# The prompt's last 24 rows at other places of VectorE's order, and another order of the sample's rounds

## The chip, the cores and the metric

One core of one Trainium2 chip runs the whole program. The metric is the device time in microseconds of one execution. The kernel before takes 2661.11 us, the median of three runs (2660.18 to 2662.83). The execution that was profiled took 2656.66 us, of which 2654.9 lie between its first and its last instruction.

## The reference, cut to what matters

One encoder layer is applied to a prompt of 256 tokens and to a sample of 512 tokens: grouped-query attention and a spatial gating unit side by side, cross attention to 256 memory rows, and then a feed-forward layer of 16384 experts, each of them one row of 1024 numbers. In each of 8 heads a token picks 16 experts out of a product of two lists of 128 keys, by two rankings:

```python
def one_block(xb):
    q = (xb @ w_q).reshape(n, PEER_HEADS, PEER_D_KEY)
    q1, q2 = jnp.split(q, 2, axis=-1)
    s1 = jnp.einsum('nhd,hkd->nhk', q1, sub_k1)        # 128 scores
    s2 = jnp.einsum('nhd,hkd->nhk', q2, sub_k2)        # 128 scores
    v1, i1 = lax.top_k(s1, 16); v2, i2 = lax.top_k(s2, 16)
    cand = v1[..., :, None] + v2[..., None, :]         # 16 x 16
    top_s, top_c = lax.top_k(cand.reshape(n, 8, 256), 16)
    idx = e1 * 128 + e2                                # the keys of top_c
    g = softmax(top_s)
    act = gelu(einsum('nhkd,nd->nhk', e_down[idx], xb))
    return einsum('nhk,nhkd->nd', g * act, e_up[idx])
```

Everything is float32, on matrix products as three products of a high and a low part.

## The kernel before, in words

Tokens lie in six tiles of 128: tiles 0 and 1 are the prompt, 2 to 5 the sample. The layer runs twice, first for the prompt, then for the sample, and then the experts of both run together. Each pass has the same stages: `mixer_inputs` (eleven column blocks), `self_attention`, `mixer_outputs` (three products of two column blocks each), `cross_inputs`, `cross_attention`, and the routing, for the sample `routing_and_gates`. Weights come in halves of a column block; ScalarE makes the high part of each (`split_hi`, L211, tile w_hi) and VectorE the low part (`split_lo`, L219, tile w_lo), for which TensorE waits. Every engine has its order of instructions written out by hand; nothing plans it at run time.

The prompt's tokens and one tile of the sample get their expert rows by gathering. The sample's other three tiles go through all 16384 experts densely, with a table of gates, "dense gates".

**The rows.** For the prompt there are 256 gathered rows of the down table, one for each of the 128 places of a token's lists and each of the two tiles, for the 128 tokens of a tile at once (512 KB). The class `Rows` holds a ring of `K = 9` slots. GpSimd asks for row r with an indirect DMA (L148) once row r - 9 has been used; VectorE takes a row with one dot product of 1024 columns for each token (L136). `bg.dve(dve, n)` puts the next n rows at this place of VectorE's order, `bg.finish` all that are left. They stand in the sample's pass as filling, from the inputs' column block 5 on. `bg.pool` lets GpSimd ask as far ahead as nine rows beyond those that VectorE takes by the end of the same stage; in the routing the function `more_rows` counts it out. The prompt's ranking is done in part of the ring's memory, before the rows begin, and in the routing four slots of the ring take scores of the sample: ScalarE waits there for 251 used rows (L1721) before it copies the third block of scores.

**The rounds.** `pick_experts(r)` ranks for unit r of the list `order`, a pair of heads c (0 to 3) of a tile t (0 to 3), four lists of 128 scores (L1834 to L1849), and in the same round ranks the candidates of unit r - 1. GpSimd adds up the candidates of a unit and looks up the keys. The scores of pair c for all four tiles come from TensorE after the query block c and are copied by ScalarE (L1714). Tiles 1, 2, 3 are the dense ones, tile 0 is gathered. When the last unit of a tile has been ranked, `shift` (L1884, L1885), an exponential on ScalarE and `finish` (L1891 to L1893) make its gates; TensorE then turns the tile (`turn_pairs`, L1682), and the dense gates can be built. They are built in 48 steps of eight token columns: VectorE writes two masks (`stamp`, L1911 and L1916), ScalarE scales one of them (`gate`, L1746, eight instructions), TensorE multiplies (L1696), ScalarE moves the result out (`unload`, L1756, two instructions), and SP stores it. Stamps stand in rounds as `aside`, six in a full one and five in the last. The experts' stage (`experts`, L2019 and on) waits for the last unload and the last store.

`keep_busy` (L250) is work without a result on TensorE.

Of the kernel before, what the change touches and what calls it, by code (L numbers as in the profile page):

```python
# [33 lines left out]
ND = 3  # L34
# [550 lines left out]
def mixer_inputs(nc, block, st, q, bg, x_in, T, Y, qT, kT, v_sb, lin, tr, A, U, GA, GS, stage, ident, gains, choice=None, norm=None, routed=None):  # L585
# [4 lines left out]
    with ExitStack() as ctx:  # L590
# [131 lines left out]
        def _(dve):  # L722
# [63 lines left out]
            def aside(c, half):  # L786
                if not q.first:
                    r = {(0, 0): 3, (1, 0): 4, (3, 0): 5, (3, 1): 6, (4, 0): 7, (4, 1): 8}.get((c, half))
                    if r is not None:
                        choice.rank(dve, r)  # L790
                    if (c, half) == (4, 1):
                        choice.shift(dve)
                    if (c, half) == (SOFTEN, 1):
                        choice.finish(dve)
                    if (SOFTEN, 0) < (c, half) < (10, 1):
                        bg.dve(dve, 5)
# [324 lines left out]
def mixer_outputs(nc, block, st, q, bg, x_in, T, Y, G, lin, tr, A, U, GA, GS, ident, cleared, attended, spills_done):  # L1121
# [3 lines left out]
    with ExitStack() as ctx:  # L1125
# [99 lines left out]
        def _(dve):  # L1225
            def each(j, oo, use):
                for c in range(2):
                    h = H + 4 * j + 2 * c
                    bg.dve(dve, 4 if (j, c) == (2, 1) else 8)
                    st.split_lo(dve, h + 2)  # L1230
                    for t in range(NT):
                        n = c * NT + t
                        dve.wait_ge(oo.ready, n + 1)
                        s = NO * j + n
                        dve.wait_ge(side_in[s % RING], 16 * (s // RING + 1))
                        use(oo, n, t, slice(c * CH, (c + 1) * CH), side[:, s % RING, :])
                        if t < NT - 1:
                            bg.dve(dve, 1)
                    st.split_lo(dve, h + 3)
                    if j == 0 and c == 0:  # L1240
                        dve.wait_ge(small_in, 48)
                        norm.dve(dve, Y, sgn[:])
# [26 lines left out]
            turn_g.dve(dve)  # L1269
            norm_m.dve(dve, M)  # L1270
# [19 lines left out]
def cross_inputs(nc, block, st, q, bg, x_in, T, Y, G, keysT, vals, lin, tr, A, ident, gains, norm_m, mixed, cleared):  # L1290
    NT, H = q.nt, q.h0 + 2 * W_XKV
    X, Y = Y, Y[:, q.t0:q.t0 + NT, :]
    with ExitStack() as ctx:
# [67 lines left out]
        def _(dve):  # L1361
# [10 lines left out]
            for h in range(10, 14):  # L1372
                bg.dve(dve, 7 if h < 13 else 3)
                st.split_lo(dve, H + h)
# [161 lines left out]
def routing_and_gates(nc, block, st, q, bg, T, Y, G, H, E12, GATE, IDX, WD, lin, tr, A, ident, gains, attended):  # L1536
# [10 lines left out]
    with ExitStack() as ctx:  # L1547
# [12 lines left out]
        begun = bg.done  # L1560
# [47 lines left out]
        order = [(c, t) for c in range(NPC) for t in (1, 2)] + [(c, 3) for c in range(NPC)] + [(c, 0) for c in range(NPC)]  # L1608
# [4 lines left out]
        AFTER = {1: 2, 2: 4 * PER_UNIT, 3: ND * OCTS - 1}  # L1613

        EARLY, ROWS_XO, ROWS_FIRST = 3, 8, 14
# [166 lines left out]
        def _(dve):  # L1782
# [112 lines left out]
            def one_row():  # L1895
                bg.dve(dve, 1)

# [22 lines left out]
            bg.dve(dve, ROWS_FIRST)  # L1920
            assert all(st.is_loaded(H0 + h) for h in range(6, 12))
            for r in range(EARLY):
                pick_experts(r, one_row)
            bg.finish(dve)
            for r in range(EARLY, 8):
                pick_experts(r)
            shift(0)
            pick_experts(8)
            finish(0)
            for r in range(9, UNITS + 1):  # L1930
                if r == 9:
                    shift(1)
                pick_experts(r, stamp)
                if r == 9:
                    finish(1)
                if r == 12:
                    shift(2)
                if r == 13:
# [11 lines left out]
        def _(pool):  # L1950
# [7 lines left out]
            taken = begun + 2 * ROWS_XO + NT - 1 + ROWS_FIRST  # L1958

            def more_rows(n):  # L1960
                nonlocal taken
                taken += n
                bg.pool(pool, min(taken + bg.K, bg.end))

            more_rows(0)
            sums = 0
            for r in range(UNITS + 1):
                u = r
                if r == EARLY:
                    bg.pool(pool, bg.end)  # L1970
                if u < UNITS:
                    if r < EARLY:
                        more_rows(4)
# [10 lines left out]
                    if r < EARLY:  # L1984
                        more_rows(1)
                u = r - 1
                if u >= 0:
# [16 lines left out]
                    if r < EARLY:  # L2004
                        more_rows(1)
# [399 lines left out]
```

## Time and profile before

| | us |
|---|---|
| median of 3 runs | 2661.11 |
| the profiled execution: time | 2656.66 |
| the profiled execution: span | 2654.9 |
| TensorE, VectorE, ScalarE, GpSimd busy | 2429.2, 2222.1, 1105.6, 1366.6 |
| mean granted clock of TensorE | 0.977 of full speed |

By stretches of the profiled execution (busy us of each engine, and the granted clock of TensorE):

| stretch, us | TensorE | VectorE | ScalarE | GpSimd | clock |
|---|---|---|---|---|---|
| 850 to 900 | 46.06 | 37.77 | 19.01 | 23.91 | 0.97 |
| 900 to 950 | 49.38 | 46.64 | 9.77 | 32.16 | 1.00 |
| 950 to 1000 | 50.00 | 41.12 | 14.29 | 21.06 | 1.00 |
| 1050 to 1100 | 48.01 | 45.03 | 19.69 | 34.80 | 1.00 |
| 1100 to 1150 | 47.67 | 38.02 | 17.85 | 36.34 | 1.00 |
| 1200 to 1250 | 48.99 | 43.35 | 20.08 | 29.71 | 1.00 |
| 1250 to 1300 | 50.00 | 43.20 | 16.21 | 34.51 | 1.00 |
| 1300 to 1350 | 36.48 | 44.91 | 11.35 | 28.94 | 0.86 |
| 1350 to 1400 | 6.40 | 48.55 | 8.18 | 23.22 | 0.52 |
| 1400 to 1450 | 30.05 | 49.42 | 46.41 | 22.45 | 0.97 |
| 1500 to 1550 | 32.09 | 49.66 | 47.49 | 20.19 | 0.93 |

The sample's attention ends near 865, its cross attention near 1177, the routing's turn near 1235, the queries near 1340; the dense gates go from 1392 to 1565, and the experts' first product starts near 1571. An engine's busy time does not say what it waits for; the chain of waits and the rows in order of time do.

### The profile page before, as it was taken

The page shows a single profiled execution, that of the slowest core. Times are in us where ns is not written, and L with a number is a line of the kernel's source. Part 1 is how long each engine was busy: PE and PEld are TensorE (multiplying, and loading weights), DVE is VectorE, ACT ScalarE, POOL GpSimd, SP SyncE. Part 2 cuts the span into 40 slices and gives each one's busy share as a digit, 9 for nine tenths or more (in the row PEclk, how much of TensorE's full clock was granted, in tenths as well). Part 3 has the DMA queues.
Part 4 walks back from the last instruction along what each step waited for, and adds up shares of the span by engine and source line. Part 5 has one row for each costly group of instructions (what it writes and reads, how often), then busy time and mean ns, then how long its engine had stood idle before and what let it go on. Part 6 is the DMA issues. An engine that isn't in the chain of part 4 may idle for free.

```text
span 2654.9 us, 38615 instructions
## 1 busy us (share of the span) xinstructions
PE 2429.2 (92%) x13259; PEld 2108.0 (79%) x13259; DVE 2222.1 (84%) x3967; ACT 1105.6 (42%) x1938; POOL 1366.6 (51%) x1054
## 2 busy tenths in 40 slices
PE   7989999899999999999916669999999999999997
PEld 5767889788866788778715559999999999989997
DVE  6355545986688888877999979999999999999998
ACT  4463444333267223333219973333333333343333
POOL 0000000326722547746654447877777777767874
PEclk9999999999999999999968999999999999999999
DMA  6735535457954988968803369999999999999996
GB/s 244 277 120 202 182 134 217 153 205 292 377 203 121 339 302 306 349 220 315 324 0 128 161 272 413 414 415 410 402 402 403 402 404 404 402 394 386 415 414 247
DMA packets 235668, 781.18 MB, mean 294 GB/s; under 512 B 21376, under 2 KB 70576, under 8 KB 214800
## 3 DMA queue, kind: packets, MB, share of 16 engines
q0 software_dynamic: 112288, 408.77, 39.6%
q1 hardware_dynamic: 123248, 370.71, 37.3%
q8 instruction: 76, 1.25, 0.2%
q14 instruction: 56, 0.46, 0.0%
HBM read 724.87 MB, written 54.53 MB: 294 GB/s over the span
## 4 chain that ended last, share of the span: by engine, by line
PE 70%; DVE 17%; ACT 5%; DMA 3%; issue 3%; POOL 2%; SPq 0%; DVEq 0%; ACTq 0%; POOLq 0%
PE lin L242 15%; PE lin L243 15%; PE lin L244 15%; PE tr L242 7%; PE tr L243 6%; PE tr L244 6%; DVE row_ring L136 2%; DVE w_lo L219 2%; DVE w_hi L1911 2%; POOL row_ring L148 1%; DVE att_nmx L1104 1%; DVE mark L1916 1%; ACT row_ring L1746 1%; ACT w_hi L211 1%; DMA w_raw<-in_wall 1%
## 5 line engine op out<-in xcount | busy, mean ns | idle before, releaser
L148 POOL DMA_INDIRECT row_ring<-in_down,IDX x256 | 366.0, 1430 | 308.9 <-DVE dots L136 235.0
L219 DVE TENSOR_TENSOR w_lo<-w_raw,w_hi 128x2048 fp32r<-128x2048 f32 x100 | 230.0, 2300 | 227.1 <-ACT w_hi L211 207.3
L242 PE MATMUL lin<-w_hi,T_hi 128*128 128x512 f32 x976 | 391.2, 401 | 15.1 <-DVE w_lo L219 7.1
L243 PE MATMUL lin<-w_lo,T_hi 128*128 128x512 f32 x976 | 387.5, 397 | 0.0
L244 PE MATMUL lin<-w_hi,T_lo 128*128 128x512 f32 x976 | 387.3, 397 | 0.0
L211 ACT ACTIVATE w_hi<-w_raw 128x2048 fp32r<-128x2048 f32 x116 | 221.9, 1914 | 353.5 <-PE lin L244 313.4
L242 PE MATMUL tr<-T_hi,w_hi 128*128 128x384 f32 x1024 | 348.8, 341 | 3.1 <-DVE w_lo L2219 3.1
L244 PE MATMUL tr<-T_hi,w_lo 128*128 128x384 f32 x1024 | 345.7, 338 | 0.0
L243 PE MATMUL tr<-T_lo,w_hi 128*128 128x384 f32 x1024 | 345.3, 337 | 0.0
L2129 POOL DMA_INDIRECT rows<-in_up,now x192 | 298.2, 1553 | 85.9 <-issue 52.7
L136 DVE CUSTOM_DVE_ANT_0 row_ring<-row_ring,H 128x1024 f32<-128x1024 f32 x256 | 306.9, 1238 | 31.2 <-DMA row_ring<-in_down,IDX 26.9
L2129 POOL DMA_INDIRECT w_raw<-in_up,now x192 | 280.4, 1461 | 87.0 <-issue 42.8
L242 PE MATMUL lin<-w_hi,c_hi 128*128 128x512 f32 x768 | 301.0, 392 | 6.7 <-issue 4.9
L243 PE MATMUL lin<-w_lo,c_hi 128*128 128x512 f32 x768 | 300.1, 391 | 0.0
L244 PE MATMUL lin<-w_hi,c_lo 128*128 128x512 f32 x768 | 299.2, 390 | 0.0
L242 PEld LDWEIGHTS lin<-w_hi,T_hi 128*128 128x128 f32 x976 | 185.1, 190 | 60.7 <-DVE w_lo L219 8.9
L2177 ACT ACTIVATE w_hi<-row_ring 128x1024 fp32r<-128x1024 f32 x128 | 135.6, 1059 | 217.0 <-PE lin L244 214.4
L244 PEld LDWEIGHTS lin<-w_hi,T_lo 128*128 128x128 f32 x976 | 185.1, 190 | 44.3
L243 PEld LDWEIGHTS lin<-w_lo,T_hi 128*128 128x128 f32 x976 | 185.4, 190 | 42.8
L2185 ACT ACTIVATE gl<-tr 128x384 f32<-128x384 f32 x128 | 62.9, 491 | 364.1 <-PE tr L244 357.7
L2246 DVE SCALAR_TENSOR_TENSOR Y<-w_raw,dots,Y 128x1024 f32<-128x1024 f32 x160 | 201.9, 1278 | 4.2 <-DMA w_raw<-in_up,now 4.1
L2246 DVE SCALAR_TENSOR_TENSOR Y<-rows,dots,Y 128x1024 f32<-128x1024 f32 x160 | 201.8, 1277 | 1.4 <-DMA rows<-in_up,now 1.3
(291 smaller groups left out, 5256.5 us busy)
## 6 DMA issues: line engine op xcount, KB each, us to landing
w_raw<-in_wall SPq DMA_DIRECT2D x116, 1024.0 KB
G<-in_downT SPq DMA_DIRECT2D x128, 512.0 KB
row_ring<-in_up SPq DMA_DIRECT2D x128, 512.0 KB
wd<-dense_gates SPq DMA_DIRECT2D x32, 768.0 KB
weight_rests<-w_lo SPq DMA_DIRECT2D x16, 1024.0 KB, 4.8
w_lo<-weight_rests SPq DMA_DIRECT2D x16, 1024.0 KB
dense_gates<-peer SPq DMA_DIRECT2D x6, 2048.0 KB, 6.7
dense_gates<-w_raw SPq DMA_DIRECT2D x6, 2048.0 KB, 7.0
```

What stands on the lines that cost most here:

```text
L136: dve.tensor_tensor_reduce(self.ring[:, k, :], self.ring[:, k, :], self.H[:, r % 2, :], 1.0, 0.0, ALU.mult, ALU.add, self.dots[:, r:r + 1] ...
L148: pool.indirect_dma_start(self.ring[:, r % self.K, :], None, self.table, bass.IndirectOffsetOnAxis(ap=self.IDX[:, r:r + 1], axis=0)).then_ ...
L211: act.activation(self.hi[:, h % 2], self.raw[:, h % 2], ACT.Copy).then_inc(self.hi_done, 1)
L219: dve.tensor_tensor(self.lo[:, h % 2], self.raw[:, h % 2], self.hi[:, h % 2].bitcast(F32), ALU.subtract).then_inc(self.lo_done, 1)
L242: pe.matmul(out, lhs[0], rhs[0], start=start, stop=False, skip_group_check=True)
L243: pe.matmul(out, lhs[0], rhs[1], start=False, stop=False, skip_group_check=True)
L244: return pe.matmul(out, lhs[1], rhs[0], start=False, stop=stop, skip_group_check=True)
L1911: dve.tensor_tensor(hot2[:, r % 4], keys[:].unsqueeze(1).broadcast_to((P, OCT, NK)), pairs[:, i, 1, OCT * r:OCT * (r + 1)].unsqueeze(2).br ...
L2129: pool.indirect_dma_start(rows[k], None, table, bass.IndirectOffsetOnAxis(ap=now[:, j % 2, k:k + 1], axis=0)).then_inc(rows_in[k], 16)
L2177: act.activation(u_hi[:, b % 2], raw_u[:, b % RAW], ACT.Copy).then_inc(u_hid, 1)
L2185: act.activation(gl[:, b % 2, :], tr[:, b % 2, 0:DENSE], ACT.Gelu_apprx_tanh).then_inc(gelued, 1)
L2246: dve.scalar_tensor_tensor(out=into, in0=rows[k], scalar=dots[:, bass.ds(first_row + r, 1)], in1=into, op0=ALU.mult, op1=ALU.add).then_inc ...
```

## The change

Rows of the prompt are counted into VectorE's order at other places. By stage, rows taken before and after: inputs 50 and 55 (also in column block 10, second half), self attention 27 and 27, outputs 62 and 74 (twelve at first instead of eight, nine instead of eight in three of the other batches, and five more ahead of the memory's norm), cross inputs 44 and 49 (7, 9, 7, 6 in place of 7, 7, 7, 3 in the last four batches), cross attention 10 and 10, the routing up to its turn 19 and 21. What is left for the time after the turn is 44 rows before and 20 after. Before, 14 of the 44 stood ahead of round 0, 17 inside rounds 0 to 2, and 13 behind them; after, all 20 stand ahead of round 0, and GpSimd asks for all of them at once, with no requests between its look-ups.

The rounds take the units in another order. Before: (c, 1) and (c, 2) for all c, then (c, 3), then (c, 0). After, tile 3 of pairs 0 and 1 stands ahead of pairs 2 and 3 of tiles 1 and 2. So tile 1 is complete with unit 8 in place of unit 6, tile 2 with unit 9 in place of unit 7; tiles 3 and 0 as before. The first tile's gates are made after round 10 (before: round 8), and stamps stand in rounds 11 to 16 (before: 9 to 16), 35 of the 48 against 47, the rest behind the last round.

```diff
-                    if (SOFTEN, 0) < (c, half) < (10, 1):
+                    if (SOFTEN, 0) < (c, half):
                         bg.dve(dve, 5)
...
-                    bg.dve(dve, 4 if (j, c) == (2, 1) else 8)
+                    bg.dve(dve, {(0, 0): 12, (1, 1): 8, (2, 1): 4}.get((j, c), 9))
...
             turn_g.dve(dve)
+            bg.dve(dve, 5)
             norm_m.dve(dve, M)
...
-                bg.dve(dve, 7 if h < 13 else 3)
+                bg.dve(dve, {11: 9, 13: 6}.get(h, 7))
...
-        order = [(c, t) for c in range(NPC) for t in (1, 2)] + [(c, 3) for c in range(NPC)] + [(c, 0) for c in range(NPC)]
+        order = [(0, 1), (0, 2), (1, 1), (1, 2), (0, 3), (1, 3), (2, 1), (2, 2), (3, 1), (3, 2), (2, 3), (3, 3)] + [
+            (c, 0) for c in range(NPC)]
...
-        AFTER = {1: 2, 2: 4 * PER_UNIT, 3: ND * OCTS - 1}
-
-        EARLY, ROWS_XO, ROWS_FIRST = 3, 8, 14
+        AFTER = {1: 2, 2: 2 * PER_UNIT, 3: ND * OCTS - 1}
+
+        ROWS_XO = 9
...
-            bg.dve(dve, ROWS_FIRST)
+            bg.finish(dve)
             assert all(st.is_loaded(H0 + h) for h in range(6, 12))
-            for r in range(EARLY):
-                pick_experts(r, one_row)
-            bg.finish(dve)
-            for r in range(EARLY, 8):
+            for r in range(ROUTED[0] + 1):
                 pick_experts(r)
             shift(0)
-            pick_experts(8)
+            pick_experts(ROUTED[1])
             finish(0)
-            for r in range(9, UNITS + 1):
-                if r == 9:
-                    shift(1)
+            shift(1)
+            for r in range(ROUTED[1] + 1, UNITS + 1):
                 pick_experts(r, stamp)
-                if r == 9:
+                if r == ROUTED[1] + 1:
                     finish(1)
-                if r == 12:
+                if r == ROUTED[2]:
                     shift(2)
-                if r == 13:
+                if r == ROUTED[2] + 1:
                     finish(2)
             shift(3)
...
-            taken = begun + 2 * ROWS_XO + NT - 1 + ROWS_FIRST
-
-            def more_rows(n):
-                nonlocal taken
-                taken += n
-                bg.pool(pool, min(taken + bg.K, bg.end))
-
-            more_rows(0)
+            bg.pool(pool, bg.end)
```

## Rows read from the trace of the kernel before

**Rows 1.** The waits from 1236 to 1400 us: engine, line, releaser, us, times, longest.

```profile
PE lin L1682 <- DVE GATE L1893: 47.4, 1, 47.4
```

**Rows 2.** VectorE in order of time, 872 to 880: start, us, instruction, idle before it.

```profile
872.60 1.22 DVE L136 CUSTOM_DVE_ANT_0 row_ring<-row_ring,H 128x1024 f32<-128x1024 f32 x1
...
873.75 1.22 DVE L136 CUSTOM_DVE_ANT_0 row_ring<-row_ring,H 128x1024 f32<-128x1024 f32 x1
...
879.80 2.29 DVE L219 TENSOR_TENSOR w_lo<-w_raw,w_hi 128x2048 fp32r<-128x2048 f32 x1 [4.82 <-issue]
```

**Rows 3.** GpSimd in order of time, two requests eight apart, 1116 to 1134.

```profile
1116.66 1.91 POOL L148 DMA_INDIRECT row_ring<-in_down,IDX  x1 [0.30 <-issue]
...
1133.04 0.94 POOL L148 DMA_INDIRECT row_ring<-in_down,IDX  x1 [0.30 <-issue]
```

**Rows 4.** VectorE in order of time, in the cross queries, 1115 to 1138.

```profile
1115.47 2.29 DVE L219 TENSOR_TENSOR w_lo<-w_raw,w_hi 128x2048 fp32r<-128x2048 f32 x1 [1.28 <-ACT w_hi L211]
...
1126.20 1.23 DVE L136 CUSTOM_DVE_ANT_0 row_ring<-row_ring,H 128x1024 f32<-128x1024 f32 x1 [1.56 <-DMA row_ring<-in_down,IDX]
...
1137.75 2.29 DVE L219 TENSOR_TENSOR w_lo<-w_raw,w_hi 128x2048 fp32r<-128x2048 f32 x1 [4.68 <-issue]
```

**Rows 5.** VectorE in order of time, four places from 745 to 992.

```profile
745.90 2.29 DVE L219 TENSOR_TENSOR w_lo<-w_raw,w_hi 128x2048 fp32r<-128x2048 f32 x1 [6.90 <-ACT w_hi L211]
...
894.65 0.17 DVE L405 RECIPROCAL sg_rstd<-sg_sd 128x1 f32<-128x1 f32 x1 [1.32 <-ACT sg_sd L390]
...
942.66 2.29 DVE L219 TENSOR_TENSOR w_lo<-w_raw,w_hi 128x2048 fp32r<-128x2048 f32 x1 [1.55 <-ACT w_hi L211]
...
991.41 0.15 DVE L400 TENSOR_SCALAR mem_ms<-mem_ss 128x1 f32<-128x1 f32 x1 [6.90 <-ACT sg_squares L386]
```

**Rows 6.** GpSimd in order of time, one request at 875.

```profile
874.98 0.94 POOL L148 DMA_INDIRECT row_ring<-in_down,IDX  x1 [0.30 <-DVE dots L136]
```

**Rows 7.** TensorE in order of time, two places where it waited for VectorE.

```profile
917.80 2.38 PE L1190 MATMUL lin<-Y,sgw 128*128 128x512 f32 x5 [0.22 <-DVE G L1246]
...
1005.99 1.38 PE L250 MATMUL lin<-ident 128*128 128x128 f32 x10 [1.66 <-DVE w_lo L219]
```

**Rows 8.** VectorE in order of time, in the routing's first product, 1200 to 1215.

```profile
1200.64 1.22 DVE L136 CUSTOM_DVE_ANT_0 row_ring<-row_ring,H 128x1024 f32<-128x1024 f32 x1 [3.11 <-DMA row_ring<-in_down,IDX]
...
1214.16 2.29 DVE L219 TENSOR_TENSOR w_lo<-w_raw,w_hi 128x2048 fp32r<-128x2048 f32 x1
```

**Rows 9.** GpSimd in order of time, one request at 1210.

```profile
1210.37 1.99 POOL L148 DMA_INDIRECT row_ring<-in_down,IDX  x1 [0.30 <-issue]
```

**Rows 10.** TensorE in order of time, the routing's transposes.

```profile
1225.80 3.71 PE L336 MATMUL lin<-ident,G 128*128 128x128 f32 x32 [1.01 <-DVE G L408]
```

**Rows 11.** VectorE in order of time, the last rows and the rounds, 1267 to 1386.

```profile
1267.41 1.23 DVE L136 CUSTOM_DVE_ANT_0 row_ring<-row_ring,H 128x1024 f32<-128x1024 f32 x1 [0.25 <-DMA row_ring<-in_down,IDX]
...
1271.89 1.21 DVE L136 CUSTOM_DVE_ANT_0 row_ring<-row_ring,H 128x1024 f32<-128x1024 f32 x1
...
1326.54 0.87 DVE L1834 MAX8 best<-G 128x8 f32<-128x128 f32 x4
...
1336.06 0.87 DVE L1834 MAX8 best<-row_ring 128x8 f32<-128x128 f32 x4
...
1385.61 0.29 DVE L1891 TENSOR_REDUCE gsum<-GATE 128x8 f32<-128x128 f32 x1
```

**Rows 12.** ScalarE in order of time, the scores of pair 1, tile 1.

```profile
1285.22 0.60 ACT L1714 ACTIVATE G<-tr 128x512 f32<-128x512 f32 x1 [3.08 <-issue]
```

**Rows 13.** ScalarE in order of time, four of the 48 gates.

```profile
1391.92 2.45 ACT L1746 ACTIVATE row_ring<-mark,pairs 128x128 f32<-128x128 bf16 x8 [2.55 <-DVE mark L1916]
...
1496.68 2.45 ACT L1746 ACTIVATE row_ring<-mark,pairs 128x128 f32<-128x128 bf16 x8 [1.59 <-DVE mark L1916]
...
1553.04 2.45 ACT L1746 ACTIVATE row_ring<-mark,pairs 128x128 f32<-128x128 bf16 x8
...
1556.33 2.46 ACT L1746 ACTIVATE row_ring<-mark,pairs 128x128 f32<-128x128 bf16 x8
```

More of the change, by code:

```diff
@@ L1559, in routing_and_gates @@
         place = m.sb("place", [P, TOPK, LOOK], BF16)
-        begun = bg.done
         OWN = bg.end % bg.K
@@ L1893, in finish @@
                 dve.tensor_tensor(v, v, total.unsqueeze(2).broadcast_to((P, PH, TOPK)), ALU.mult).then_inc(softened, 1)
-            def one_row():
-                bg.dve(dve, 1)
             stamps = 0
@@ L1968, in _ @@
                 u = r
-                if r == EARLY:
-                    bg.pool(pool, bg.end)
                 if u < UNITS:
-                    if r < EARLY:
-                        more_rows(4)
                     pool.wait_ge(halved, u + 1)
@@ L1983, in _ @@
                     pool.tensor_copy(id_b[:, u % 3], ids[:, u % 2]).then_inc(ids_read, 1)
-                    if r < EARLY:
-                        more_rows(1)
                 u = r - 1
@@ L2003, in _ @@
                                        x[:, 0], x[:, 1], ALU.add).then_inc(looked_up, 1)
-                    if r < EARLY:
-                        more_rows(1)
         def gated_all(eng):
```

## The prediction

> **What bounds the kernel now.** I read the busy shares by slice first, then the table by stage, the waits of the stage in which TensorE goes thin, and last each engine's instructions in order of time around every place that the change touches. Three stretches come out. In the front (to 1326 us) TensorE is over 90% busy, so whatever makes it wait there adds its whole length. From 1326 to 1390 TensorE is idle: its longest wait is for VectorE's line 1893, the gates of the first dense tile [rows 1]. From 1392 to 1565 ScalarE builds the dense gates, and the experts behind it (1084 us) start when it is done. So two things count: how late the front gets, and when round 10's tile is ready.
>
> **The rows in the front.** A row is one VectorE dot product over 1024 columns, and a run of them steps by 1.15 us [rows 2]. Rows come through a ring of nine, so only nine can be ready when a run starts. The tenth must be asked for by GpSimd when a slot comes free. Eight requests on end took 16.4 us, 2.05 each [rows 3], and from request to use it was 9.5 us where the transfer ended the wait (1116.66 in [rows 3], 1126.20 in [rows 4]). The new counts, by place:
>
> - Column block 10 of the sample's inputs, +5 rows, 5.7 us. VectorE idles 6.90 us there for ScalarE's weight half [rows 5], and all nine are ready. Cost 0 (0 to 1).
> - First batch before the attention output, 8 to 12. The run now ends where the w_lo split starts after 4.82 us of idleness [rows 2], which would hold 4.6 us. But three rows are beyond the nine, and the last of them is the request of 874.98 [rows 6]. It lands at 884.5 by the 9.5 us, so the split ends at 887.8, TensorE's next half waits half a microsecond, and four additions (0.6 each) and three rows put the next split's end near 895.9. ScalarE's root makes VectorE wait 1.32 us until 894.65 [rows 5], which takes most of this: 1.2 us late (0 to 2.5).
> - Second batch, 8 to 9. TensorE's spatial product at 917.80 waits for the last gated addition [rows 7], so this is 1.15 us in full. Both together: +2.4 (1.15 to 3.5).
> - Gate output, first batch 8 to 9: before its split lie 1.55 us of idleness [rows 5]. Cost 0.
> - Five rows before the memory's norm: 5.7 us in a gap of 6.90 us [rows 5]. Hidden, but their five replacements are fetched beside the memory rows for which that gap waits, 0 to 1 us; I take 0.6. The batch behind it goes from 8 to 9, and its split is what TensorE waits for at 1005.99 [rows 7]: 1.15 in full. Together +1.7 (1.15 to 2.5).
> - Cross queries, 7, 7, 7, 3 to 7, 9, 7, 6. Two more rows before a split with 1.28 us of idleness [rows 4] cost TensorE nothing by themselves, for the split is needed later. But GpSimd is the pacer here: the 21st row, asked for at 1116.66, is used at 1126.20 after a wait for its transfer. It stays 21st of the run, now with two more behind it before the third split: that split runs from 1129.6 to 1131.8, and six rows follow. By VectorE alone they end at 1138.7. The 29th is asked for at 1133.04 [rows 3] and lands at 1142.5 by the 9.5 us, at 1140 by 7. The last split starts at 1137.75 now [rows 4], and the first maximum of cross attention waits for it. So +0.95 by VectorE alone, +5.9 by the longest latency; I take +3.2, with the fetches less crowded once the projections' weights are in.
> - Query projection, first stage of the routing, 8 and 8 to 9 and 9. At its start nine are ready, so nine fit. The rows between the tile additions now are the ones that had to be asked for: the wait of 3.11 us before 1200.64 [rows 8] comes one tile earlier, and each later row stands two requests further back. The last of the second nine is the request of 1210.37 [rows 9]. It is ready at 1216.4 at best and 1219.9 by the 9.5 us, so the split that starts at 1214.16 [rows 8] starts at 1217.6 or later. The two additions and squares behind it move along, and with them the last normed tile, for which TensorE waits at 1225.80 [rows 10]. VectorE alone would make it 1.0 late (of 2.3 us more rows, 1.3 go into its waits for TensorE's tiles); I take +3.2 (1.0 to 5).
>
> The front is later by 2.4 + 1.7 + 3.2 + 3.2 = 10.5 us (4.3 to 15). SP's and GpSimd's queues keep their orders; only the requests' times move.
>
> **The rounds.** All times here are before the shift of 10.5. Of 44 rows after the routing's turn, 20 stay, now in one run before round 0. The 18th of them waits for its transfer and is used at 1267.41 [rows 11]; two more follow at 1.15 us, so the run ends at 1270.9. Round 0 has no second stage: five passes over four rankings, of which the first kind takes 0.87 us [rows 11], 5.2 us with the links between them (an estimate). Round 1 is a full one, 9.52 us, the distance of the round starts at 1326.54 and 1336.06 [rows 11]. That gives 1285.6. Round 2 is now head pair 1 of tile 1; its scores are copied at 1285.22 to 1285.82 [rows 12]. So round 2 starts at 1285.9, by both. The later scores are no wait: rounds 6 and 8 need head pairs 2 and 3 at 1324 and 1343, and a column block takes TensorE about 26 us (96 products of 0.23 us and the scores, an estimate), so they come near 1311 and 1337; the ring's slots into which they go are free by 1271.
>
> Before, rounds 3 to 8 and the shift of tile 1's gates ran from 1326.54 to 1385.61 [rows 11], 59.1 us. After, rounds 2 to 10 and the same shift take 59.1 + 3 x 9.52 = 87.6 us from 1285.9, which ends at 1373.5. **Gain 12.1 us** (10 to 13). What goes is 24 rows (27.5 us) and most of their waits; what comes is two more rounds before the first gates (19 us), which the later stretch gets back, since it has two fewer.
>
> **The dense gates.** There are 48 eights of columns. ScalarE takes 3.29 us for each when nothing holds it (1553.04 to 1556.33), but in the rounds with six stamps VectorE paces it: 1391.92 to 1496.68 is 30 eights less one, 3.61 us each [rows 13]. Before, seven rounds went like this; after, five do, and the other 18 eights go at ScalarE's pace: 18 x 3.29 = 59.2, and 2.4 for the exchange of tiles, which fell in slack before (an estimate). So 104.8 + 61.6 = 166.4 us from first to last gate, against 1391.92 to 1556.33 and one more of 3.4, 167.8. **Gain 1.4 us** (0 to 4). VectorE's 13 stamps without a round cost it 1.8 us each, well below 3.29, and hide.
>
> **Sum.** 10.5 - 12.1 - 1.4 = -3.0 us. The profiled execution has a span of 2654.9 and a time of 2656.66 (1.76 around it), and becomes 2653.7. The median of the runs shown, 2661.11, lies 4.45 above the profiled execution; with the 3.0 off, the forecast is 2658.1.
>
> **A rule against the row.** The one request that matters most is shown: 9.5 us from request to use at 1116.66 [rows 3, 4]. By the Trainium skill (DMA: Bandwidth & Descriptors, Anatomy of one DMA — SWDGE (gpsimd) path) a transfer asked for by GpSimd takes about 2.0 us and its bytes at 436 GB/s, which makes an estimate of 3.2 us for a row's 512 KB. The trace does not agree, as the queue is full here. By that rule every extra row would be ready in time and the front would cost what VectorE alone makes it; that is the first rival.
>
> **Rivals.** *The front rows are nearly free.* Transfers land well under 9.5 us after their request, and the idle places (4.82, 4.68 us) take the rows. For it: each gap is about as long as its new rows. Against it: 1126.20 and 1200.64 already wait for a transfer before rows are added. The front then costs 1.15 + 1.15 + 0.95 + 1.0 = 4.3, and the sum is -9.2: 2651.9.
>
> *The run of 20 rows starves (slower).* Place: the one wait between the turn and round 0. The 18th row still waits for its transfer at 1267.41, so fetches are far behind here; if the 19th and 20th each come two requests' time (4.1 us) after the row before, the run ends at 1276.8. Each microsecond past 1270.9 is lost in full, and from 3.0 us on the change loses. Price 5.9: the sum is +2.9, 2664.0; with the front at its upper end beside it, past 2667. Against it: the old order used its 20th row at 1271.89 without a wait [rows 11].
>
> *The new order does not pay.* If tile 1's gates had been held by something other than VectorE's rounds, only the front's lateness and the 1.4 would stay: +9, 2670. The wait of 47.4 us on line 1893 speaks against it [rows 1].
>
> **How the numbers follow.** I give the forecast case 0.55 (its own range 2654 to 2661: the four front terms within 1.5 each), the free front 0.27, the starved run 0.12, the last 0.06. About 0.2% (5.3 us) is what a measurement can tell from no change. Faster by more than that: the second case nearly whole and a fifth of the first, 0.36. Slower: half of the starved run and the last case, 0.12. Same: 0.52. For 8 in 10 the range must take in most of the free front and the edge of the starved run: 2650 to 2665.
>
> **What would show it.** Right: TensorE's transposes of the routing (1225.80) about 10 us later; a wait for a transfer at the end of the cross queries' last six rows and of the second nine; TensorE's spatial product about 2 us later; the last prompt row near 1281, 45 us earlier than now; round 2's first maximum within 1 us of ScalarE's copy; line 1893 first near 1384 (1373.5 + 10.5); the experts 3 us earlier. Wrong: the front under 5 us late, which makes the first rival, or the twentieth row ending more than 2 us after 1270.9 plus the shift. An experts stage of another length than 1084 us would be outside all of this.

## The result, and the profile after

The changed kernel takes 2666.98 us, the median of 20 runs (2662.21 to 2668.93), against 2658.78 for the kernel before (20 runs). The medians are 8.2 us apart; the ratio is 1.0024, with a 95% interval of 1.0017 to 1.0031, so the change makes the kernel slower by 4.5 to 8.2 us. The forecast was 3.0 us faster, 2658.1, with a range of 2650 to 2665, and the result lies above it. (The median of 2661.11 that the forecast started from was of three runs and 2.3 us above that of the 20.) The profiled execution of the changed kernel has a span of 2665.8 us, 10.9 more than before.

The waits of TensorE from 860 to 1400 us in the changed kernel (engine, line, releaser, us, times, longest; a line number from 1270 to 1900 is one higher than before):

```profile
PE lin L1683 <- DVE GATE L1894: 41.5, 1, 41.5
PE lin L891 <- DVE xatt_probs L955: 7.3, 1, 7.3
PE lin L336 <- DVE G L408: 3.6, 1, 3.6
PE lin L1190 <- DVE G L1246: 3.1, 1, 3.1
PE lin L250 <- DVE w_lo L219: 2.9, 1, 2.9
```

The idle time for the first gates [rows 1] became only 5.9 us shorter, and four waits ahead of it, in a stage where TensorE has no slack, grew: before the cross attention's transposes (1.6 us before, in two waits), before the routing's (1.0) [rows 10], before the spatial product (0.2) and before the gate output's second block (1.7) [rows 7].

VectorE of the changed kernel in order of time (start, us, instruction, idle before it and what ended it):

```profile
883.77 1.23 DVE L136 CUSTOM_DVE_ANT_0 row_ring<-row_ring,H 128x1024 f32<-128x1024 f32 x1 [5.37 <-DMA row_ring<-in_down,IDX]
...
887.55 2.29 DVE L219 TENSOR_TENSOR w_lo<-w_raw,w_hi 128x2048 fp32r<-128x2048 f32 x1
...
1135.60 1.23 DVE L136 CUSTOM_DVE_ANT_0 row_ring<-row_ring,H 128x1024 f32<-128x1024 f32 x1 [1.66 <-DMA row_ring<-in_down,IDX]
...
1151.27 1.23 DVE L136 CUSTOM_DVE_ANT_0 row_ring<-row_ring,H 128x1024 f32<-128x1024 f32 x1 [4.78 <-DMA row_ring<-in_down,IDX]
...
1153.57 2.29 DVE L219 TENSOR_TENSOR w_lo<-w_raw,w_hi 128x2048 fp32r<-128x2048 f32 x1
...
1229.98 1.23 DVE L136 CUSTOM_DVE_ANT_0 row_ring<-row_ring,H 128x1024 f32<-128x1024 f32 x1 [1.17 <-DMA row_ring<-in_down,IDX]
...
1256.62 1.22 DVE L1812 TENSOR_TENSOR H<-G,pairs 128x1024 f32<-128x1024 f32 x1
...
1291.43 0.87 DVE L1835 MAX8 best<-G 128x8 f32<-128x128 f32 x4
...
1307.85 0.87 DVE L1835 MAX8 best<-G 128x8 f32<-128x128 f32 x4 [1.71 <-ACT G L1715]
...
1395.49 0.29 DVE L1892 TENSOR_REDUCE gsum<-GATE 128x8 f32<-128x128 f32 x1
```

They answer to [rows 2, 4, 8, 11]. A row of the first batch waits 5.37 us for its transfer, and the split of 879.80 is 7.75 us late; the last split of the cross queries (1137.75 before) is 15.8 us late, after a wait of 4.78 for a transfer. Round 0 begins at 1291.43, round 2 at 1307.85, and the gates of tile 1 come at 1395.49 instead of 1385.61.

ScalarE of the changed kernel, the copy that round 2 waits for, the first eight of dense gates and the last (before: [rows 12, 13]):

```profile
1307.17 0.60 ACT L1715 ACTIVATE G<-tr 128x512 f32<-128x512 f32 x1 [3.07 <-PE tr L1663]
...
1401.79 2.44 ACT L1747 ACTIVATE row_ring<-mark,pairs 128x128 f32<-128x128 bf16 x8 [2.54 <-DVE mark L1914]
...
1569.95 2.52 ACT L1747 ACTIVATE row_ring<-mark,pairs 128x128 f32<-128x128 bf16 x8
```

Executions of one kernel differ by a few us ahead of all that was changed, so places are compared from a common mark: VectorE's last subtraction of self attention. In the kernel before and in the changed one it is

```profile
863.98 0.69 DVE L1099 TENSOR_TENSOR T_lo<-tr,T_hi 128x512 fp32r<-128x512 f32 x1 [3.02 <-ACT T_hi L1078]
```

```profile
865.28 0.69 DVE L1099 TENSOR_TENSOR T_lo<-tr,T_hi 128x512 fp32r<-128x512 f32 x1 [3.13 <-ACT T_hi L1078]
```

so 1.3 of the 10.9 us lie ahead of it. All kernels of this study, in us behind the mark of their own profiled execution (the last column is VectorE's first instruction of the experts' stage):

| kernel | rows left, from H | first maximum, cross attention | H written | last row's end | gates of tile 1 | first dense gate | experts |
|---|---|---|---|---|---|---|---|
| before | 44, among rounds | 276.0 | 371.3 | 462.6 | 521.6 | 527.9 | 701.2 |
| changed | 20 | 290.5 | 391.3 | 426.2 | 530.2 | 536.5 | 710.1 |
| old_order | 20 | 290.6 | 392.1 | 426.6 | 519.6 | 525.9 | 699.5 |
| hid_old | 33 | 278.8 | 375.9 | 437.6 | 520.9 | 527.2 | 700.7 |
| hid_new | 33 | 277.3 | 373.4 | 434.1 | 536.4 | 542.7 | 715.2 |
| counts_old_new_order | 44 | 276.2 | 371.7 | 452.7 | 554.9 | 561.2 | 733.7 |
| before_hidden | 33, among rounds | 277.3 | 373.5 | 446.1 | 505.0 | 511.3 | 683.1 |
| filled | 20 | 286.3 | 389.9 | 424.5 | 528.9 | 535.2 | 707.4 |
| no_cross | 25 | 284.1 | 384.3 | 429.7 | 532.0 | 538.3 | 710.6 |
| no_00 | 25 | 287.4 | 389.0 | 435.8 | 538.1 | 544.4 | 715.5 |
| no_xo | 22 | 290.4 | 389.9 | 428.7 | 531.0 | 537.3 | 710.4 |

H is the normed token tile that L1811 (L1812) writes just before the routing's rows. Every line of the table is one execution, and kernels whose front is the same differ in it: H is at 371.3 and 371.7 in two kernels with the old counts, and at 372.3 and 375.3 in two more that come below (`half_dot`, `half_fetch`); with eleven rows moved it is at 373.4, 373.5 and 375.9. So differences in H of less than some 4 us say little by themselves. The 10.9 us of span are then: the front +20.0 (H), the rest up to tile 1's gates -11.4, the dense gates +0.3, the experts +0.7 (2654.9 - 863.98 - 701.2 against 2665.8 - 865.28 - 710.1), the mark +1.3.

### The profile page after: what moved, and what is told of

The parts are those of the page before. It is cut to its first block, busy times and chain, and to the rows that moved or that the text cites. A ratio compares the mean times of both kernels' runs of the same rounds, so it can differ in the third digit from the quotient of the medians.

```text
span 2665.8 us, 38614 instructions
## 1 busy us (share of the span) xinstructions
PE 2436.4 (91%) x13259; PEld 2113.7 (79%) x13259; DVE 2216.4 (83%) x3967; ACT 1107.5 (42%) x1938; POOL 1357.0 (51%) x1054
## 4 chain that ended last, share of the span: by engine, by line
PE 67%; DVE 19%; ACT 6%; issue 3%; DMA 3%; POOL 2%; SPq 0%; DVEq 0%; ACTq 0%; POOLq 0%
PE lin L242 14%; PE lin L243 14%; PE lin L244 14%; PE tr L242 7%; PE tr L243 6%; PE tr L244 6%; DVE row_ring L136 3%; DVE w_lo L219 2%; ACT row_ring L1747 2%; POOL row_ring L148 2%; DVE att_nmx L1104 1%; DMA row_ring<-in_down,IDX 1%; DVE w_hi L1909 1%; ACT w_hi L211 1%; DMA w_raw<-in_wall 1%
## 5 line engine op out<-in xcount | busy, mean ns | idle before, releaser
L2108 POOL DMA_INDIRECT w_raw<-in_up,now x192 | 287.1, 1495 | 86.7 <-issue 45.7
L242 PEld LDWEIGHTS lin<-w_hi,T_hi 128*128 128x128 f32 x976 | 185.5, 190 | 64.6 <-DVE w_lo L219 10.9
L2164 ACT ACTIVATE gl<-tr 128x384 f32<-128x384 f32 x128 | 62.9, 492 | 371.7 <-PE tr L244 362.2
```

The lines of the kernel that those rows point to most:

```text
L242: pe.matmul(out, lhs[0], rhs[0], start=start, stop=False, skip_group_check=True)
L2108: pool.indirect_dma_start(rows[k], None, table, bass.IndirectOffsetOnAxis(ap=now[:, j % 2, k:k + 1], axis=0)).then_inc(rows_in[k], 16)
L2164: act.activation(gl[:, b % 2, :], tr[:, b % 2, 0:DENSE], ACT.Gelu_apprx_tanh).then_inc(gelued, 1)
```

## Experiments

**Order and counts apart.** Four kernels: old or new order, and three sets of counts. The old order put back in the changed kernel (`old_order`):

```diff
-        order = [(0, 1), (0, 2), (1, 1), (1, 2), (0, 3), (1, 3), (2, 1), (2, 2), (3, 1), (3, 2), (2, 3), (3, 3)] + [
-            (c, 0) for c in range(NPC)]
+        order = [(c, t) for c in range(NPC) for t in (1, 2)] + [(c, 3) for c in range(NPC)] + [(c, 0) for c in range(NPC)]
...
-        AFTER = {1: 2, 2: 2 * PER_UNIT, 3: ND * OCTS - 1}
+        AFTER = {1: 2, 2: 4 * PER_UNIT, 3: ND * OCTS - 1}
```

Expected: 

> The rows of the changed kernel, the old order of the rounds. Theory A (the loss is the front's 21 us of lateness, the rounds went as forecast, and the new order costs two rounds before the first gates): front as in the changed kernel (routing's transposes near 1245, rows' run ends near 1291). Rounds 2, 4 and 6 may wait for scores copied at 1307.2, 1329.4 and 1353.4; round 6 starts near 1354 and the gates of tile 1 come after three rounds and the shift (30.6 us), near 1385, 11 us before the changed kernel's 1395.5; the gates' stretch stays at 168 us. Time about 11 us under the changed kernel, that is 2654 to 2658, no slower than before. Rival B (the new order is what pays): later rounds wait longer for scores or the dense gates get slower by seven rounds with stamps, and the time is at or above the changed kernel's 2667.

Measured: 2655.51 us, 0.9989 of the kernel before (0.9979 to 1.0000), that is 11.5 under the changed kernel. (All ratios are to the kernel before, run beside the experiment; its medians there are 2658.39 to 2659.68.) VectorE of `old_order`, rounds 2, 4 and 6:

```profile
1307.07 0.88 DVE L1834 MAX8 best<-G 128x8 f32<-128x128 f32 x4 [1.66 <-ACT G L1714]
...
1332.92 0.87 DVE L1834 MAX8 best<-row_ring 128x8 f32<-128x128 f32 x4 [6.87 <-ACT row_ring L1714]
...
1353.27 0.87 DVE L1834 MAX8 best<-row_ring 128x8 f32<-128x128 f32 x4 [1.36 <-ACT row_ring L1714]
```

Rounds 4 and 6 now wait 6.87 and 1.36 us for scores, which the new order avoids, but the first gates need two rounds (19 us) fewer. The gates come 10.6 us earlier by the table, and the dense stretch with seven stamped rounds is as long as with five (173.6 us from first gate to experts in both). Theory A holds.

The counts (`counts_old_new_order` puts all of them back, `hid_old` and `hid_new` keep eleven rows in the front, `hid_old` with the edit of `old_order` beside it and `hid_new` with the new order):

```diff
-                    if (SOFTEN, 0) < (c, half):                                # counts_old_new_order only
+                    if (SOFTEN, 0) < (c, half) < (10, 1):
...
-                    bg.dve(dve, {(0, 0): 12, (1, 1): 8, (2, 1): 4}.get((j, c), 9))
+                    bg.dve(dve, 4 if (j, c) == (2, 1) else 8)                  # counts_old_new_order
+                    bg.dve(dve, {(1, 0): 9, (2, 1): 4}.get((j, c), 8))         # hid_old, hid_new
...
-            bg.dve(dve, 5)                                                     # counts_old_new_order only
...
-                bg.dve(dve, {11: 9, 13: 6}.get(h, 7))
+                bg.dve(dve, 7 if h < 13 else 3)
...
-        ROWS_XO = 9
+        ROWS_XO = 8
```

Expected: 

> Only the 11 rows that I held to be covered stay in the front (five in column block 10, one in the gate output's first batch, five before the memory's norm); old order of the rounds; 33 rows in one run in the routing. Theory A: the routing's transposes come within 2 us of 1225.8 of before, the run starts near 1236 and ends at 1285 to 1293, round 6 starts at 1338 to 1346, tile 1's gates at 1369 to 1377 against 1385.6 before: 9 to 17 us faster than before, 2642 to 2650. Rival C (those rows aren't covered, or 33 rows in one run starve): the transposes come 5 us late or more, or the run ends after 1300, and the gain is under 3 us.

Expected: 

> The front as before, the new order of the rounds, all 44 rows in one run ahead of round 0. Theory A: the front's lateness goes wholly (transposes at 1225.8 within 1 us), the run of 44 ends at 1298 to 1312, two rounds of 14.7 us and 87.6 us to tile 1's gates follow: 1400 to 1414, 15 to 28 us later than before; 2673 to 2687. Rival B (order pays by itself): under 2662.

Expected: 

> The 11 covered rows in the front, 33 in the routing's run, the new order. Theory A: tile 1's gates 19 us later than in the kernel with the same rows and the old order (two rounds more), less what that one waits for scores: 1387 to 1397 against 1385.6 before, so 2660 to 2670, within 4 us of the changed kernel. Rival B (the new order pays): at least as fast as the same rows with the old order.

Measured: `hid_old` 2656.60 us, 0.9991 (0.9982 to 1.0000); `counts_old_new_order` 2692.09, 1.0132 (1.0116 to 1.0147); `hid_new` 2672.13, 1.0056 (1.0042 to 1.0069). H and the first maximum of round 0 on VectorE, first in `hid_old`, then in `counts_old_new_order`:

```profile
1239.47 1.22 DVE L1811 TENSOR_TENSOR H<-G,pairs 128x1024 f32<-128x1024 f32 x1
...
1301.18 0.87 DVE L1834 MAX8 best<-G 128x8 f32<-128x128 f32 x4
```

```profile
1236.87 1.22 DVE L1811 TENSOR_TENSOR H<-G,pairs 128x1024 f32<-128x1024 f32 x1
...
1317.77 0.87 DVE L1834 MAX8 best<-G 128x8 f32<-128x128 f32 x4
```

The order again: with the same rows the old one is 15.5 us faster. The eleven rows are nearly covered: H is at 371.3 to 375.3 with none of them and at 373.4 to 375.9 with all. But my expectation of 2642 to 2650 for `hid_old` was wrong, by the run; the other two times lie above theirs as well (2673 to 2687 and 2660 to 2670), the run of 44 with an end at 1317.9 instead of 1298 to 1312. Counted from H, 33 rows on end take 61.7 us in `hid_old`, 44 take 81.0, 25 take 45.4 (`no_cross`) or 46.8 (`no_00`), and 20 take 34.9. Behind the first twenty, a row costs 1.9 to 2.4 us, not the 1.15 of [rows 2].

**The same 33 rows among the rounds** (`before_hidden`): the kernel before, its order and its rows between the passes of rounds 0 to 2, with only the eleven rows moved.

```diff
-                    if (SOFTEN, 0) < (c, half) < (10, 1):
+                    if (SOFTEN, 0) < (c, half):
...
-                    bg.dve(dve, 4 if (j, c) == (2, 1) else 8)
+                    bg.dve(dve, {(1, 0): 9, (2, 1): 4}.get((j, c), 8))
...
+            bg.dve(dve, 5)
             norm_m.dve(dve, M)
```

Expected: 

> The kernel before with its rows among the first three rounds and its order; only 11 rows moved to the covered places (five in column block 10, one in the gate output's first batch, five before the memory's norm), so 33 in the routing and only two of them behind round 2. Theory A (a row in one run costs 2.0 us, the pace of its request and transfer, but 1.15 where it stands between a round's passes): transposes near 1226, round 3 starts near 1306 instead of 1326.5, round 6 is held by the scores of head pair 3 near 1338, tile 1's gates near 1369: about 15 us faster than before, 2641 to 2647. Rival C (rows among the rounds are paced as in one run): round 3 starts at 1316 or later, gates near 1379, 2651 to 2655.

Measured: 2642.45 us against 2659.02 for the kernel before, 0.9944 (0.9931 to 0.9958). VectorE, rounds 0, 3 and 6 and the gates of tile 1:

```profile
1257.23 0.87 DVE L1835 MAX8 best<-G 128x8 f32<-128x128 f32 x4 [1.93 <-ACT G L1715]
...
1305.05 0.86 DVE L1835 MAX8 best<-G 128x8 f32<-128x128 f32 x4
...
1333.49 0.87 DVE L1835 MAX8 best<-row_ring 128x8 f32<-128x128 f32 x4
...
1364.01 0.29 DVE L1892 TENSOR_REDUCE gsum<-GATE 128x8 f32<-128x128 f32 x1
```

The last row ends 8.5 us later than in `hid_old` (446.1 against 437.6), but by then three rounds are done instead of none; tile 1's gates come 15.9 us earlier, the whole kernel 14 us. Most of the three rounds' passes (some 24 us, 5.2 and 2 x 9.52 in the prediction) fit into the rows' waits, and the change gave that place away. This is the fastest version of the study, 24.5 us under the changed kernel.

**What paces a run.** Two kernels on `counts_old_new_order`, one with half the bytes for the last 35 rows, one with half the VectorE work for the last 44. Both leave something out, half of each row or half of each product, and so compute something else.

```diff
+            w = D // 2 if r >= 221 else D        # half_fetch: GpSimd's request of columns 0:w of the slot
...
+            w = D // 2 if r >= 212 else D        # half_dot: VectorE's product over columns 0:w
```

Expected: 

> The kernel with all 44 rows in one run (81 us, 1.84 a row), in which the last 35 rows' requests fetch 256 KB instead of 512 (so the dots are of other numbers); VectorE's instructions stay. Theory V (the run is paced by the volume that the queues move, 1.25 us a row and the projection's weights beside it): the run falls to 53 to 62 us, near VectorE's 1.15 a row. Theory P (it is paced by GpSimd's requests at 1.25 to 2.0 us and a fixed time from request to landing): 74 to 80 us.

Expected: 

> The same run of 44 with full fetches, in which VectorE's product of each of the last 44 rows goes over 512 columns instead of 1024 (0.6 us instead of 1.2). Theory V: the run stays within 3 us of 81. Theory P2 (VectorE's reading is what stretches GpSimd's requests from 0.95 to 1.98 us, and the requests pace the run): requests of 0.95 throughout and a run under 70 us.

Measured (2681.18 us, 1.0077 with 1.0061 to 1.0092; 2684.94 us, 1.0100 with 1.0084 to 1.0116): the run of 44 takes 69.1 us with half the bytes and 74.5 with half the product, against 81.0. So the run's length lies outside what either theory gave, in both, and neither cause holds alone. GpSimd's requests from 1240 to 1300 by line (count | busy us, mean ns | idle before), and one stretch of the table by stage (its last three columns: granted clock, busy share of the DMA engines, GB/s), of `counts_old_new_order`, `half_fetch` and `half_dot`:

```profile
L148 POOL DMA_INDIRECT row_ring<-in_down,IDX x32 | 39.3, 1227 | 36.5 <-DVE dots L136 29.4 <-issue 7.0
...
1260.00:1280.00 20.00, 20.00 (x101) 16.71 (x100) 10.56 (x18) 5.91 (x9) 12.08 (x12) 1.00 1.02 423
```

```profile
L149 POOL DMA_INDIRECT row_ring<-in_down,IDX x33 | 49.3, 1495 | 25.4 <-DVE dots L136 15.7 <-issue 9.8
...
1260.00:1280.00 20.00, 20.00 (x100) 16.72 (x100) 13.11 (x24) 5.40 (x7) 16.34 (x13) 1.00 0.87 325
```

```profile
L149 POOL DMA_INDIRECT row_ring<-in_down,IDX x32 | 30.2, 944 | 26.2 <-DVE dots L137 23.7 <-issue 2.4
...
1260.00:1280.00 20.00, 20.00 (x100) 16.75 (x99) 7.01 (x21) 7.20 (x9) 8.83 (x10) 1.00 1.02 420
```

With full rows the DMA engines are full (1.02, 423 GB/s; rows and the query projection's weights together). They are as full with half products (1.02, 420 GB/s), so there the transfers are what is left. With half rows they are not (0.87), and GpSimd's requests, 1495 ns on average, are the next limit: they follow one another with 0.30 us between, and the request of 1258.99 in `half_fetch` comes 7.4 us after the end of the product (1250.36 to 1251.58) that frees its slot. The requests are long while VectorE is in a product and 944 ns throughout when its products are half as long. So there are two limits close to one another, and taking one away shows the other. By the Trainium skill (SBUF — State Buffer, Who interferes with whom) a VectorE instruction with two SBUF inputs and a GpSimd instruction that reads SBUF lock each other out, the later one waits for the whole of the earlier. The trace agrees for the full products: requests (which read their row numbers, IDX, from SBUF) of 0.94 and 1.91 to 1.99 us, 1.0 apart, near the product's 1.15; that the half ones lengthen no request at all it does not explain.

**TensorE's clock** (`filled`): the changed kernel with spare products in the four waits.

```diff
-            keep_busy(pe, lin[:, 5], ident, 0.0 if q.first else 6.3)
+            keep_busy(pe, lin[:, 5], ident, 0.0 if q.first else 9.1)
...
-                    keep_busy(pe, tr[:, 1], ident, 1.8)
+                    keep_busy(pe, tr[:, 1], ident, 8.4 if bg.end else 1.8)
...
+                           early=None if q.first else lambda: keep_busy(pe, tr[:, 0], ident, 2.5)   # ahead of the second block's wait
...
-            keep_busy(pe, lin[:, 5], ident, 2.9)
+            keep_busy(pe, lin[:, 5], ident, 6.1)
```

Expected: 

> The changed kernel with spare products on TensorE in the four waits that came new or grew (2.8 us before the spatial product, 2.5 before the second column block of the gate output, 6.6 before the cross attention's transposes, 3.2 before the routing's). The waits themselves stay. Theory D (after each of them the profile grants 0.50 for some 3 to 4 us, which costs 1.6 to 2.4 us each): granted clock 1.00 behind all four, the routing's first row 4 to 6 us earlier than 1257.8, tile 1's gates and the time 4 to 6 us earlier: 2661 to 2663. Rival E (the clock costs nothing that counts, the lateness is VectorE's alone): time within 1 us of the changed kernel, or longer by fills that overrun.

Table by stage of the changed kernel, behind the wait of 3.1 us for the spatial product, and then of `filled` at the same place and around the fourth wait (PE busy, PEld, DVE, ACT, POOL, granted clock, DMA share, GB/s):

```profile
922.00:924.00 2.00, 1.52 (x3) 0.80 (x4) 2.00 (x2) 0.00 (x0) 1.69 (x2) 0.74 0.99 369
924.00:926.00 2.00, 2.00 (x4) 0.85 (x3) 1.40 (x3) 0.00 (x0) 1.70 (x2) 0.50 1.08 410
926.00:928.00 2.00, 2.00 (x5) 0.76 (x4) 1.41 (x3) 0.00 (x0) 1.55 (x2) 0.91 0.92 367
```

```profile
920.00:926.00 6.00, 6.00 (x37) 4.45 (x36) 6.00 (x9) 0.00 (x0) 5.28 (x3) 1.00 0.98 391
...
1240.00:1246.00 6.00, 1.88 (x14) 1.69 (x13) 4.24 (x11) 2.96 (x9) 0.42 (x1) 0.86 0.89 365
1246.00:1252.00 6.00, 6.00 (x32) 5.96 (x31) 4.45 (x6) 4.73 (x8) 0.00 (x0) 0.57 0.01 5
```

In the changed kernel the clock goes to 0.50 of full speed, that is 1.2 GHz, behind the wait, and is back after some 3.5 us. Behind the wait of 2.9 us it is the same (1015 to 1018.5), and at those of 7.3 and 3.6 us it is at 0.50 for nearly 7 us, the first part of them still idle (1155 to 1162, 1244 to 1251). With the fill it stays at 1.00 at the first three places; at the fourth the fill ended too early and a wait of 4.1 us stayed, with 0.57 behind it. Time: 2663.90 us, 1.0010 (1.0000 to 1.0020), some 3 us less than the changed kernel, with intervals that still overlap a little. Behind the mark, the first maximum of cross attention is 4.2 us earlier and the first addition of the routing 5.3 (339.0 against 344.3), but H only 1.4, which is less than such tables tell apart. What takes the difference are two waits of VectorE in `filled`, with the rows now asked for no earlier:

```profile
1212.33 1.23 DVE L136 CUSTOM_DVE_ANT_0 row_ring<-row_ring,H 128x1024 f32<-128x1024 f32 x1 [5.84 <-DMA row_ring<-in_down,IDX]
...
1228.79 1.22 DVE L136 CUSTOM_DVE_ANT_0 row_ring<-row_ring,H 128x1024 f32<-128x1024 f32 x1 [3.21 <-DMA row_ring<-in_down,IDX]
```

Theory D holds for the clock, but its price in the time was put too high: a part is given back to the rows.

Such a stretch also comes behind shorter waits, and not every time. In the kernel before there is one right behind the common mark, after a wait of 2.00 us; in the changed kernel the wait there is 2.12 us and the clock stays at 1.00:

```profile
866.00:868.00 2.00, 2.00 (x6) 1.61 (x5) 2.00 (x3) 0.00 (x0) 1.69 (x1) 0.50 0.92 321
```

```profile
866.00:868.00 2.00, 1.98 (x9) 1.62 (x10) 2.00 (x3) 0.00 (x0) 0.62 (x1) 1.00 0.89 306
```

It moves TensorE's spatial product: where eight rows stand in each of the two batches ahead of it, that comes 53.7 to 53.8 us behind the mark in the five kernels that have the stretch, and at 52.2 in the three that have not (`no_00`, `half_fetch`, `half_dot`). This is a part of the spread of H.

**Single places of the front.** `no_cross` has `7 if h < 13 else 3`, `no_00` has `{(0, 0): 8, (0, 1): 8, ...}`, and `no_xo` has `ROWS_XO = 8`, each in the changed kernel.

Expected: 

> The changed kernel with the cross queries' rows back at 7, 7, 7, 3: five rows more in the routing's run. Theory A: cross attention's first maximum and all behind it 6.5 to 9 us earlier than in the changed kernel (forecast term: 3.2), the run of 25 rows 10 us longer at 2.0 us a row; tile 1's gates 1 to 4 us later, 2667 to 2671. By the forecast's terms (3.2 in the front, 1.15 a row) the gates would come 2.6 us later as well, but the first maximum only 3.2 earlier: the place of the maximum tells them apart.

Expected: 

> The changed kernel with the attention output's batches back at 8 and 8 (12 and 9): five rows more in the routing's run. Theory A with D: TensorE's spatial product at 918 instead of 922.5, no half clock behind it, so 5 to 6 us earlier by 935 (forecast term: 2.4); the run 10 us longer; tile 1's gates 3 to 6 us later than in the changed kernel, if nothing between takes up the 5 us. Without D: 3.5 us earlier by 935.

Expected: 

> The changed kernel with 8 and 8 rows in the routing's first stage instead of 9 and 9. Forecast term 3.2: the routing's run starts 3.2 us earlier than 391.3 us behind the attention's end, and is two rows longer (2 to 4 us). In the trace of the changed kernel the stretch from that stage's first addition to the run's start is 4.4 us longer than before, 1.7 of it at half clock; so 3 to 4.4 earlier by that. The time within 2 us of the changed kernel either way.

`no_cross`: 2667.33 us, 1.0034 (1.0021 to 1.0048). The first maximum is 6.4 us earlier (284.1 against 290.5), H 7.0; the run of 25 is 10.5 us longer. The upper value held, not the forecast's 3.2. `no_00`: 2671.88 us, 1.0052 (1.0038 to 1.0066). TensorE's wait for the spatial product goes back to 0.3 and the norm of the memory is 6.4 us earlier (126.3 against 132.7), as expected, but H only 2.3: the waits before the gate output's second block (4.0), the cross attention (6.2) and the routing (5.3) take the rest. Its run of 25 takes 46.8 us, and tile 1's gates come 7.9 us later than in the changed kernel, where 3 to 6 were expected. `no_xo`: 2662.65 us, 1.0012 (1.0003 to 1.0021). From the routing's first addition to H it takes 42.6 us, as before, against 47.0: 4.4 less, as expected. In its profiled execution that addition came 3 us later than in the changed kernel, though nothing ahead of it differs, so the table shows no gain. Part of that is the clock again: behind a wait of 2.01 us at 1193 it is at 0.50 in `no_xo` and stays at 1.00 in the changed kernel. As its run of 22 rows takes 4.0 us more than that of 20, a time within 2 us was expected; that the median is 4 us lower stays unexplained.

## Why the prediction was wrong

**The front: 10.5 forecast, 20.0 measured.** This is the term that failed, by two steps: the cross queries were put at 3.2 us and took 6.4, and what TensorE's clock does behind a wait was put at nothing and took 6.3. In its parts:

- First two batches, forecast 2.4: 3.4 up to the spatial product. The nature was right (the rows beyond the nine wait for transfers, 5.37 us at 883.77), the size at least 1 us short. The 3.4 has luck in it: the profiled execution of the kernel before lost some 1.6 us at this place to the half clock behind the mark. Against the 52.2 of `no_00` it is 5.0, beyond the upper bound of 3.5.
- TensorE's clock behind that wait: not in the forecast. 1.9 us from the spatial product to the memory's norm (75.5 us against 73.6), which `filled` takes back (73.6). The same behind the wait before the gate output's second block (1.6), behind the one in cross attention (1.1, from the first maximum to the routing's first addition, 53.8 us against 52.7, and 52.7 in `filled`) and behind the one before the routing's transposes (1.7; there `filled` did not keep the clock up, and `no_xo`, whose wait is 1.0 us, shows none). These 6.3 us are two thirds of the miss of 9.5. They are terms of a sum and not what a cure brings: with the first three gone in `filled`, H came only 1.4 us earlier. I had priced each wait at its length. The kernel covers its known waits with `keep_busy`, and behind the waits of [rows 7] (0.22 and 1.66 us) the granted clock was 1.00; the question of what a wait of 3 us does to it was never asked. By the Trainium skill (TensorE: Matmul & The Clock Gate, Part 1) idleness throttles the engine and work releases it, and the trace agrees: 0.50 behind each of the four waits, 1.00 where three of them were filled.
- The five rows before the memory's norm and the batch behind it, forecast 1.7: 1.2. Right within its size.
- Cross queries, forecast 3.2: 6.4, shown by `no_cross`. The bounds were 0.95 and 5.9, and I took the middle because the fetches would be less crowded. They were not: the wait before 1151.27 is 4.78 us, and from its request (1140.82) to its use it was 10.4 us. The longest latency seen was the value to take; by it the forecast would have been 5.9.
- The routing's first stage, forecast 3.2: 2.7, and 4.4 with the clock, which `no_xo` shows.

**The run of 20 rows: right.** 34.5 us forecast from first row to last, 33.8 measured (1257.76 to 1291.5). It was right only at this length. The rival of a starved run did not occur here, but did at 25 and more.

**The rounds: right, 12.1 forecast, 11.4 measured.** Round 2 starts 0.68 us after the copy of its scores does, and from it to tile 1's gates it takes 87.64 us against 87.6. (That TensorE is idle from 1326 us, as the prediction says at its start, is misread: the wait of [rows 1] begins at 1340.4 and ends at 1387.8. No term of the sum hangs on it.) But two comparisons that I did not make were worth more than the sum. The two rounds that the new order puts ahead of the first gates were said to be got back by the later stretch, which has two fewer, though the sum gives that stretch only 1.4 us. `old_order` shows that nothing comes back: the two rounds cost 10.6 us there, and 15.5 between `hid_old` and `hid_new`. And rows among rounds 0 to 2 cost less than rows ahead of them, 15.9 us for 33 rows.

**The dense gates: gain 1.4 forecast, 0.3 lost.** From the first gate to the last it is 168.2 us (1401.79 to 1569.95), where I forecast 166.4. The last twelve eights go at 3.31 us each, as forecast; the 35 steps before them take 128.5 us, where the forecast's terms give 126.8. Seven stamped rounds (`old_order`) and five give the same stretch to the experts.

The sum with the measured terms is 20.0 - 11.4 + 0.3 = +8.9, with 0.7 in the experts and 1.3 ahead of the mark 10.9 in span. The last two are within what executions differ by. Of the rivals, the free front is excluded. The one called "the new order does not pay" gave 2670 and came nearest, for another reason than the one that held: tile 1's gates do hang on VectorE's rounds, and the new order costs two of them.

## What to carry to other kernels

A wait that you add to a saturated TensorE costs its length, and behind it can come a stretch at half clock (1.1 to 1.9 us here), so ask of each new wait of 2 us or more what the engine does in it. Work moved out of a late stage into an early one is free only where the trace shows idleness and the data are already there; in a run that is paced by requests and transfers count the run by their pace (here 2 us a row), not by the consumer's instruction. And where items are paced by something else, put independent work between them: the same 33 rows were 14 us cheaper among the rounds than ahead of them.

## What the runs showed of the hardware

- GpSimd's request for a gathered row took 0.94 us in half products (mean 944 ns of 32) and often 1.9 to 2.0 us beside products of 1024 columns.
- Rows of 512 KB came so late that VectorE stepped by 1.9 to 2.4 us a row behind the first twenty of a long run, at 423 GB/s with the weights beside them; halving the bytes brought the 44 rows from 81.0 to 69.1 us only, halving the products to 74.5.
- TensorE's granted clock was 0.50 for some 3.5 to 7 us at idle stretches of 2.9 to 7.3 us, and 1.00 where these were filled with spare products. At waits of 2.0 to 2.2 us it was 0.50 in some executions and 1.00 in others.
